# A sixth place for expert weights, and the second layer's filter and modulation work done inside the first layer

## What is computed

```python
for l in range(2):
    mod = (silu(c) @ ada_w[l] + ada_b[l])            # 1024 x 6144 matrix, one row of input
    sh1, sc1, g1, sh2, sc2, g2 = split(mod, 6)       # six vectors of 1024
    h = rms_norm(x, ln1_g[l]) * (1 + sc1) + sh1
    cols = h @ w_in[l]                               # 1024 x 2464, four groups a, b, c, d
    # a: latent attention, b: windowed attention, c: differential attention
    # d: two long convolutions (FFT) with filters that do not depend on x:
    #    f = sin(.. sin(.. sin(z @ w1 + b1) @ w2 + b2) @ w3 + b3)   (512 x 64)
    #    filt = (f @ w4) * window ; normalised by its sum of squares over time
    x = x + g1 * (concat(a, b, c, d) @ w_out[l])
    h = rms_norm(x, ln2_g[l]) * (1 + sc2) + sh2
    # 32 experts of 1024 -> 256 -> 1024 (gate, up, down); each token goes to 2 of them
    x = x + g2 * moe(h)
out = rms_norm(x, final_g)
```

## Time and profile before

| | |
|---|---|
| median of 3 runs | 1728.01 us (1724.51 to 1730.16) |
| profiled execution, its own time | 1733.8 us |
| its span in the profile | 1732.0 us |
| TensorE busy | 1393.2 us, 80% of the span |
| VectorE busy | 617.7 us, 36% |
| ScalarE busy | 369.5 us, 21% |
| moved by DMA | 335.53 MB |
| mean granted TensorE clock | 0.916 of full speed |

### The profile page before, as it was taken

How to read it: one execution, slowest core, us unless ns; L and a number is a source line. 1 busy time by engine, 2 the same in 40 slices (tenths; PEclk the granted TensorE clock), 3 DMA queues, 4 the chain that set the end, 5 groups by cost and what they waited for, 6 DMA issues and landing times.

```text
span 1732.0 us, 18436 instructions
## 1 busy us (share of the span) xinstructions
PE 1393.2 (80%) x6748; PEld 788.4 (46%) x6748; DVE 617.7 (36%) x1444; ACT 369.5 (21%) x832; POOL 265.8 (15%) x250
## 2 busy tenths in 40 slices
PE   2789999898798697887778999989879869877742
PEld 0244655565443454444424465556544345444421
DVE  3352523357723421232135252335772342111111
ACT  0221111545402110111022111154540211111101
POOL 0000300000001252332200030000000125323211
PEclk9779999999998799999967999999999879999976
DMA  7511030461145499999851103045114649999932
GB/s 244 227 71 49 33 113 16 146 196 50 52 174 227 170 331 404 409 404 404 312 220 71 48 34 112 16 146 195 49 53 171 231 170 353 402 401 406 393 137 110
DMA packets 98152, 335.53 MB, mean 194 GB/s; under 512 B 28310, under 2 KB 33046, under 8 KB 72816
## 3 DMA queue, kind: packets, MB, share of 16 engines
q1 hardware_dynamic: 74688, 305.48, 45.2%
q0 software_dynamic: 15072, 16.85, 4.3%
q10 hardware_dynamic: 8304, 12.03, 2.0%
HBM read 324.04 MB, written 27.80 MB: 203 GB/s over the span
## 4 chain that ended last, share of the span: by engine, by line
PE 65%; DVE 13%; ACT 7%; issue 6%; DMA 5%; POOL 2%; SPq 1%; POOLq 0%; DVEq 0%; ACTq 0%
PE bank L469 60%; ACT pr_r L1259 2%; PE bank L718 2%; PE bank L813 2%; DMA big<-in_moe_w_down_dram 2%; DVE pr_r L1866 2%; DMA big<-in_ada_w_dram 1%; DVE pr_r L1727 1%; ACT pr_r L1306 1%; DVE pr_r L1869 1%; PE bank L568 1%; POOL small L1366 1%; SPq L932 1%; ACT ht_r L1238 1%; DVE small L1725 1%
## 5 line engine op out<-in xcount | busy, mean ns | idle before, releaser
L469 PE MATMUL bank<-big,pr_r 128*64 128x256 f32 (+2 forms) x3272 | 465.2, 404 | 95.9 <-issue 53.1
L469 PEld LDWEIGHTS bank<-big,pr_r 128*64 128x64 f32 (+1 forms) x3272 | 283.5, 152 | 250.2 <-issue 144.9
L469 PE MATMUL bank<-big,ht_r 128*128 128x512 f32 (+2 forms) x832 | 329.9, 547 | 1.5 <-ACT ht_r L1272 1.5
L469 PEld LDWEIGHTS bank<-big,ht_r 128*128 128x128 f32 x832 | 155.0, 190 | 144.4 <-issue 138.0
L469 PE MATMUL bank<-big 128*128 128x256 f32 (+4 forms) x528 | 196.9, 516 | 25.7 <-ACT big L1243 10.6
L1430 POOL DMA_INDIRECT x_rows<-ht_r,slot_i x64 | 101.8, 1590 | 341.8 <-DVE ht_r L1872 306.4
L469 PEld LDWEIGHTS bank<-big 128*128 128x128 f32 (+2 forms) x528 | 104.0, 208 | 86.1 <-issue 41.5
L1866 DVE TENSOR_TENSOR pr_r<-pr_r,bank 64x256 f32<-64x256 f32 x65 | 27.5, 423 | 278.1 <-ACT pr_r L1306 266.3
L1306 ACT ACTIVATE pr_r<-bank 64x256 f32<-64x256 f32 x64 | 24.2, 378 | 442.3 <-PE bank L469 442.3
L1872 DVE SCALAR_TENSOR_TENSOR ht_r<-bank,mix_r,mod 128x512 f32<-128x512 f32 x65 | 48.8, 751 | 132.6 <-PE bank L469 132.6
L1365 POOL TENSOR_SCALAR small<-small 128x1 f32<-128x1 f32 (+2 forms) x20 | 6.9, 346 | 579.6 <-DVE small L1752 326.6
(11 more groups left out here) (272 smaller groups left out, 1220.6 us busy)
## 6 DMA issues: line engine op xcount, KB each, us to landing
big<-in_moe_w_gate_dram SPq DMA_DIRECT2D x65, 1024.0 KB, 15.3
big<-in_moe_w_up_dram SPq DMA_DIRECT2D x65, 1024.0 KB, 21.2
big<-in_moe_w_down_dram SPq DMA_DIRECT2D x65, 1024.0 KB, 26.4
big<-in_ada_w_dram SPq DMA_DIRECT2D x16, 3072.0 KB, 11.5
big<-in_w_in_dram SPq DMA_DIRECT2D x4, 3072.0 KB, 15.5
big<-in_w_out_dram SPq DMA_DIRECT2D x4, 2048.0 KB, 7.9
mod<-in_ada_b_dram SPq DMA_DIRECT2D x12, 512.0 KB, 10.1
big<-in_w_in_dram SPq DMA_DIRECT2D x2, 2048.0 KB, 8.0
```

What stands on the lines that cost most here:

```text
L469: return nc.tensor.matmul(o, l, r, start=start, stop=stop)
```

## The change

- **Sixth place.** A slot 5 lies where `x_tok` (gate, up) and the first two rows of `mod` (down) are. It is used once per layer, by expert 5; SyncE issues its load when the eight row groups of h are made and `x_tok` has been stored to `x_rows`. From expert 6 on the four slots go round.
- **Modulation sums of layer 1.** Its chunks 0 to 2 ("next") are loaded and summed in the attention of layer 0, after outputs 25, 30 and 35; the layer's own five chunks stand at 3, 7, 11, 16, 20. ScalarE stores `part` (times 32) to a tensor in device memory, `ada_rows`, and SyncE reads one row of each group of 32 back in the expert stage. At the start of layer 1 six products with four rows of ones remain.
- **Filter stage of layer 1.** It becomes 17 jobs behind experts of layer 0 (`JOBS`): the three network layers behind 12, 14 and 16, eight half rows behind 17 to 24, four squares behind 25 to 28, the sum behind 29 and the scale behind 31. The filter rows are put where `x_tok` lies. So `x_tok` is loaded back in layer 1 only when the filter transforms have read them: tiles 0 and 1 after `fco1`, 2 and 3 after `fdo1`. SyncE waits for the scatters there, not for `moe_done`, when there is no further round.
- The load of filter tensors moves from behind expert 9 to behind expert 11.

```diff
-        MLP_AT = {14: 0, 18: 1, 22: 2}
-        MOD_AFTER = {3: 3, 8: 4, 13: 5, 18: 6, 23: 7}
+        JOBS = {12: ("net", 0), 14: ("net", 1), 16: ("net", 2), 29: ("sum",), 31: ("scale",)}
+        JOBS.update({17 + i: ("row", i // 2, i % 2) for i in range(2 * NT)})
+        JOBS.update({17 + 2 * NT + t: ("square", t) for t in range(NT)})
+        MOD_AFTER = [{3: ("ada", 3), 7: ("ada", 4), 11: ("ada", 5), 16: ("ada", 6), 20: ("ada", 7),
+                      25: ("next", 0), 30: ("next", 1), 35: ("next", 2)},
+                     {3: ("ada", 3), 8: ("ada", 4), 13: ("ada", 5), 18: ("ada", 6), 23: ("ada", 7)}]
...
+        CHUNKS = [[("ada", c) for c in range(3)] + IN + LATE + [("next", c) for c in range(3)] + OUT, IN + LATE + OUT]
...
-        EXPERT_SLOT = [2, 3, 0, 1, 4] + [(2, 3, 1, 0)[i % 4] for i in range(NE - 5)]
+        EXPERT_SLOT = [2, 3, 0, 1, 4, 5] + [(2, 3, 0, 1)[i % 4] for i in range(NE - 6)]
...
         def expert_slot(s):
+            if s == 5:
+                return at(x_flat, 0, KT, F), at(x_flat, KT * F, KT, F), mod[:, 0:2, :]
...
+                    pe.wait_ge(parts_in, 16 * 3)
+                    for c in range(3):
+                        for half, (lo, n) in enumerate(((0, 512), (512, 256))):
+                            mm(V.bank(f"m{c}{half}")[:, 0:n], ones[0:4, :], next_parts[c][:, lo:lo + n]).then_inc(ready_v, 1)
+                    pe.wait_ge(job_taken_v, sum(not a for a in by_scalar.values()))
...
                     down(b, s).then_inc(y_done, 1)
-                    if e in MLP_AT and l + 1 < DEPTH:
+                    if e in JOBS and l + 1 < DEPTH:
+                        next_filter(bank[4 + b], *JOBS[e]).then_inc(job_done, 1)
...
+                def next_filter(b, what, *which):
+                    if what == "row":
+                        t, d = which
+                        pe.wait_ge(mlp_ready, 3 * (l + 1) + 3)
+                        return mm(b[:, :], mlp_h[:, t * P:(t + 1) * P], w4[:, d * S:(d + 1) * S])
+                    if what == "square":
+                        t = which[0]
+                        pe.wait_ge(sq_ready, NT * (l + 1) + t + 1)
+                        for i in range(2):
+                            last = mm(b[32 * t:32 * t + 32, :], ones[:, 0:32], sq_next[:, i], i == 0, i == 1)
+                        return last
...
+                    else:
+                        sp.wait_ge(hrow_ready, 2 * NT * (l + 1))
+                        sp.wait_ge(x_stored, 16 * NT * (l + 1))
...
-                    if e == 9 and l + 1 < DEPTH:
+                    if e == 11 and l + 1 < DEPTH:
                         load_filters(l + 1)
                         load_mods(l + 1)
...
-                    sp.wait_ge(y_done, NE * l + last_in_slot(0) + 1)
-                    load_chunk(0, l + 1)
+                    sp.wait_ge(y_done, NE * l + last_in_slot(1) + 1)
+                    load_chunk(IN[0], l + 1)
                     sp.wait_ge(y_done, NE * l + last_in_slot(2) + 1)
                     load_waves()
-                    sp.wait_ge(y_done, NE * l + last_in_slot(1) + 1)
-                    load_chunk(1, l + 1)
...
                 for t in range(NT):
+                    if l + 1 < DEPTH:
+                        done(sp, "fco1" if t < 2 else "fdo1")
                     sp.dma_start(x_tok[:, t, :], x_rows[t * P:(t + 1) * P, :]).then_inc(x_in[t], 16)
...
+                    if kind == "next":
+                        act.wait_ge(taken_a, R.n)
+                        act.dma_start(ada_rows[c], part[:, :]).then_inc(ada_stored, 16)
...
+                    elif what == "row":
+                        t, d = which
+                        fs, fd_ = fsum_of[l + 1][:, t], fdif_of[l + 1][:, t]
+                        TT(two(f_other if d else fs), two(b[:, :]), win(t), ALU.mult).then_inc(job_taken_v, 1)
+                        if d:
+                            v.wait_ge(job_taken_v, n)
+                            step(TT(fd_, fs, f_other, ALU.subtract))
+                            TT(fs, fs, f_other, ALU.add).then_inc(filt_ready, 1)
```

More of the change, by code:

```diff
@@ L429, in chunk_used @@
                 done(eng, f"p{which}1")
+            elif kind == "next":
+                done(eng, f"n{which}1")
             elif kind == "out":
@@ L515, in layer @@
[L515 to L531, removed]
-                pe.wait_ge(srep_ready, l + 1)
-                b = V.bank("fnb")
-                for j in range(4):
-                    last = mm(b[:, j * P:(j + 1) * P], f_tmp[:, j * P:(j + 1) * P], ident[:, :])
-                last.then_inc(ready_v, 1)
@@ new lines, in layer @@
+                    b = A.bank("fp")
+                    for t in range(NT):
+                        if t + 1 < NT:
+                            filter_rows(t + 1)
+                        pe.wait_ge(sq_ready, NT * l + t + 1)
+                        for i in range(2):
+                            last = mm(b[32 * t:32 * t + 32, :], ones[:, 0:32], squares[t % 2][:, i], i == 0, i == 1)
+                        if t < 2:
+                            last.then_inc(sq_used, 1)
+                    last.then_inc(ready_a, 1)
@@ new lines, in layer @@
+                    mod_parts_sum("ada", 2)
+                    taken(pe, "fp")
+                    b = V.bank("fn")
+                    for j in range(4):
+                        last = mm(b[:, j:j + 1], f_tmp[:, j * P:(j + 1) * P], ones[:, 0:1])
+                    last.then_inc(ready_v, 1)
+                    pe.wait_ge(srep_ready, l + 1)
+                    b = V.bank("fnb")
+                    for j in range(4):
+                        last = mm(b[:, j * P:(j + 1) * P], f_tmp[:, j * P:(j + 1) * P], ident[:, :])
@@ L693, in layer @@
                 taken(pe, "cT3")
-                for what, n in steps:
+                for what, n in steps_of[l]:
                     if what == "S":
```

340 lines of the change are left out of this document (211 added, 129 removed).

## The result

The changed kernel takes 1676.8 us (median of 4 runs, 1673.9 to 1683.3) against 1728.3 (1724.5 to 1730.2): ratio 0.971, 95% interval 0.968 to 0.974. I had forecast 1680, with a range of 1665 to 1698. The profiled execution has a span of 1676.7 us (its own time 1678.5), against 1732.0.

A forecast was written before the change was run, and what follows sets the result against it. Expert stages were taken as bound by TensorE's ring early, by weight loads later. Attention +8.0, layer 0's experts −7.6, between layers −40, layer 1's experts −9.0: −48.6 from 1728.0 gives 1679.4, said as 1680, range 1665 to 1698.

The forecast's parts named there:

- Attention of layer 0: Three more chunks of modulation sums there lengthen it by 2 × 2.8 + 2.4, together +8 us, bounds 0 to 9.
- Sixth place: Expert stage of each layer: expert 5's load is hidden and engines idle less; −9.0 us per layer, bounds 5 to 11.
- the count of work up to expert 10's slot: Expert stage: DMA work fills 42.2 of the 42.9 us until slot 2 returns, leaving new idle 0.7 plus the ramp.
- Jobs: Layer 0's expert stage: filter work fits TensorE's 1.57 us wait per expert except squares, 0.3 over each; +1.4 us.
- not above 9: Sign: in layer 0, experts 17 to 28 keep a spacing near 8.7 us, not above 9.
- rival (b): Layer 0's second half bound by TensorE's ring, jobs cost up to 17 us instead of 1.4; 1693 us, chance 0.10.
- Rival (d): Behind each job the next expert waits for the whole detour, 2.9 or 3.9 us per job; slower, 1746, chance 0.02.
- Between the layers: From layer 0's last down product to layer 1's first projection 45.5 us instead of 85.5; −40 us, bounds 34 to 45.
- nothing there changes: Between the layers: VectorE still begins 10.1 us after layer 0's last down product, behind the last scatter.
- rival (c): Shorter transition: quicker loads and clock recovery, −45 us between the layers and 11 per layer; 1667 us, chance 0.10.
- Layer 1 ahead of its experts: Attention of layer 1 was forecast to take the same time as before.
- Rival (a): Expert stages: engines idle later instead, only 0 to 2 us gained per layer; 1695 us, chance 0.17.

The follow-up runs named there:

- place only: The kernel before with the sixth place alone, for expert 5, and some filter, modulation and router loads moved; 1708.0 us, 0.988.
- more places: The changed kernel with places reused: all six in turn in layer 1, the sixth for experts 10 and 14 in layer 0; some loads moved; 1672.5 us, 0.965.
- five places: The changed kernel without the sixth place, so expert 5 waits for a slot; all jobs stay; 1687.6 us, 0.976.
- jobs twice: The changed kernel with each product of the eight row jobs and four square jobs made twice; 1689.9 us, 0.976.
- jobs out: The changed kernel without rows, squares, sum and scale behind layer 0's experts; 1642.1 us, without the overflow block in layer 1; layer 0's stage 265.0.
- Chunk at end: The changed kernel with layer 1's second input weight chunk loaded right behind layer 0's last down product, not behind the transforms; 1681.2 us, 0.972.
- order only: The kernel before, its five places going round as 2, 3, 0, 1 up to expert 24, not 2, 3, 1, 0; 1723.0 us, 0.996.

## Why the prediction was right, and where its terms were off

The total was right: by the spans −55.3 us, by the medians −51.4, where the sum said −48.6. That it came so near has some luck in it: the terms were off by up to 4.3 us each, to both sides. Its terms, from the table:

- *Attention of layer 0*, +8.0: measured +7.1 (C to expert 0). By the start of expert 0 it looks like 5.5, because C itself came 1.6 us sooner. The prices 2.8, 2.8, 2.4 were wrong one by one: 1.2 or nothing for the first, 5.9 for two. The pair of rows in group a could price the sum, not the places.
- *Sixth place*, −9.0 per layer: −8.4 and −6.8 (place only against before). What I had counted as one thing are two. The end of the idle time of expert 7's slot, for which I took 3.7, came from the order of the places: 2.1 and 3.5. The place itself, 7.4 − 1.8 = 5.6 in the sum, gave 6.3 and 3.3. The step that failed is the count of work up to expert 10's slot. It found the 42.9 us filled but for 0.7 and the ramp; 4.3 us stayed idle in layer 0 and 4.6 in layer 1. In layer 1 7.4 − 4.6 = 2.8 is about what was gained, and more places, where this idle time goes, gives 5.0 back and so shows that it was on the path. Which part of the count was too high is not shown; the likeliest is the remainder for table writes, which I had worked out as a difference and not read from a row. Why layer 0 gained 6 us in spite of its 4.3 idle stays open: five places and the changed kernel, with all other loads in the same order, part by 6 us at experts 11 to 13 there.
- *Jobs*, +1.4: measured 0 within 1 us (263.4 with the place alone, 263.6 and 264.6 with place and jobs). The mechanism was the one forecast, waits turned into work; 16 us in them stand against my 17 without cover. The pace is 8.36 us for rows and 9.1 for squares, so my sign "not above 9" failed for the squares. Behind them and behind most rows there is no wait left: TensorE's ring with its jobs sets the pace there, which is the mechanism of rival (b), at a price within what a stage varies. A row costs 1.2 us over the ring's 7.15 and a square 2.0, a bit over 0.93 and 1.86. With 1.9 us of waits left behind rows, jobs that lengthen the stage were near: jobs twice is that case. Rival (d), 2.9 or 3.9 us per job, is refuted by these 1.2 and 2.0 us and by jobs out, whose stage is no shorter.
- *Between the layers*, −40: −44.3. The step that failed is "nothing there changes" of the last scatter. Something did: before, a chunk of `ada_w` was issued at 856.64 into the scatter, and the change issues no load there (in both the waves, issued earlier, are still landing). Chunk at the end puts one there and gets 2.7 of the 3.7 us back. The load there is of 1664 KB, the one before was of 3072, which may be the remaining 1.0; no run shows it. Counted from VectorE's start the other terms held within about 1 us: transforms for 15.5 us instead of 16.7, VectorE at its rows from T + 28.0 instead of 32.3, the third of them 0.6 late for `x_tok`, and 5.25 us from the last row to the projection. The bound of 45 us (rival (c)) was nearly reached, though by this, and by the clock of the execution compared with, not by quicker loads. (Rival (c)'s own terms, 45 and 11 per layer with 8 for attention and 1.4 for jobs, make about 1670 and not the 1667 that I wrote.)
- *The clock*: I had compared with one execution whose filter rows ran at the lower level (0.50 of full speed). By order only and place only, some 3 to 6 us of that stretch come and go with it, so a part of the 44 us is no lasting gain. It would fit that the profiled execution of before was 5.5 us above its median and that of the change 1.7, which is why the medians give 51.4 and the spans 55.3; the stretches of the other executions are not on record.

- *Layer 1 ahead of its experts*: forecast the same, measured 464.6 and 462.5 us; the other kernels, some with before's code there, lie between 462.5 and 463.3, so this is variation of one or two us.

Rival (a), idle engines later, holds in mechanism in both layers: 4.3 and 4.6 us idle, about half of the 16 that it would have taken from the sum.

## What to carry to other kernels

Here work put where an engine waits for weights was free as long as such waits were left beside it, and then cost its full time; the list of waits with the work left out and with it doubled finds both ends. Before a buffer is added, look at the order in which the present ones are handed on: here a swap of two numbers in a table gave half of what the new buffer seemed to give in layer 1, and there using the places again gave more (5.0 us) than adding one (3.3). Two chunks of products cost 5.9 us between the short steps of attention, and nothing that could be measured in one long wait (9.57 us) a little later. Before a difference in a stretch is put down to an edit, compare the granted clock in it.

## What the runs showed of the chip

A scatter-add of an expert's 128x512 output from GpSimd took 3.66 us from issue to landing at a DMA share of 0.21 (expert 31 of layer 1, changed kernel), 4.65 at 0.33, 7.32 at 0.79 with a load of 1664 KB issued just ahead of it, and 8.28 at 1.01 with one of 3072 KB (expert 31 of layer 0, before). A stretch whose code was untouched was 3.4 and 6.6 us shorter in two other kernels, most of it with the moment at which TensorE's granted clock rose again from 0.50 to 1.00.
